# Prompt scores of a differential attention: one 128-row matmul against zero-padded queries, or two 64-row tiles of the array in turn

## What is computed

```python
scale = HEAD_DIM ** -0.5                          # HEAD_DIM = 64, N_SUB = 8, N_HEADS = 4
s = jnp.einsum('bqhd,bkhd->bhqk', q_blk, k, preferred_element_type=jnp.float32) * scale
s = jnp.where(k_pos[None, :] <= q_pos[:, None], s, -jnp.inf)
p = jax.nn.softmax(s, axis=-1)                    # per sub-head
a = p[:, :, 0] - lam * p[:, :, 1]                 # the two sub-heads of a head
out = jnp.einsum('bhqk,bkhe->bqhe', a, v)         # v: 4 heads of 128
```

## Time and profile before

| | |
|---|---|
| median of 3 runs | 1545.1 us (1535.18, 1545.1, 1546.49) |
| span of the profiled execution, first to last instruction | 1539.1 us |
| PE busy | 1306.9 us, 85% of the span |
| PE weight loads busy | 883.9 us, 57% |
| DVE busy | 744.7 us, 48% |
| ACT busy | 568.3 us, 37% |
| POOL busy | 283.7 us, 18% |
| mean granted TensorE clock | 0.937 of full speed |

### The profile page before, as it was taken

The page is one execution under the profiler, slowest core; times in us unless marked ns, Lnnn a source line. Parts: engine busy times, 40 slices in busy tenths (PEclk is TensorE's granted clock), DMA queues, the critical chain, the costliest instruction groups (busy, mean ns, idle before and its releaser), DMA issues.

```text
span 1539.1 us, 20098 instructions
## 1 busy us (share of the span) xinstructions
PE 1306.9 (85%) x5769; PEld 883.9 (57%) x5770; DVE 744.7 (48%) x1101; ACT 568.3 (37%) x786; POOL 283.7 (18%) x289
## 2 busy tenths in 40 slices
PE   4879999999997799789999899638989989899920
PEld 1334444366665466566565688426767777677720
DVE  4863232201113887511011454567865556888747
ACT  4530111000001556422232122206755546777633
POOL 0020000010000111000000011112554344554424
PEclk9989999999998999999999899758999999999965
DMA  8981200011100200077664311406875765888545
GB/s 288 367 318 32 82 28 26 16 46 42 41 0 0 84 1 1 1 233 237 193 173 126 127 41 42 183 16 247 303 269 200 272 251 218 313 303 324 216 157 184
DMA packets 84544, 230.86 MB, mean 150 GB/s; under 512 B 16101, under 2 KB 28517, under 8 KB 72165
## 3 DMA queue, kind: packets, MB, share of 16 engines
q1 hardware_dynamic: 70288, 203.80, 37.6%
q0 software_dynamic: 14192, 26.24, 4.8%
HBM read 220.42 MB, written 34.21 MB: 165 GB/s over the span
## 4 chain that ended last, share of the span: by engine, by line
PE 64%; DVE 10%; DMA 9%; issue 7%; ACT 5%; POOL 2%; DVEq 2%; ACTq 1%; SPq 1%; POOLq 0%
PE psum L530 19%; PE psum L583 12%; PE psum L611 11%; PE psum L690 4%; DMA xg<-h_scratch,gidx 4%; PE psum L517 4%; PE psum L705 2%; PE psum L629 2%; DMA wada<-in_w_ada_dram 2%; PE psum L638 2%; DVE xgL L1493 1%; ACT pexp L922 1%; DVEq L332 1%; PE psum L672 1%; DMA wgu<-in_w_up_dram 1%
## 5 line engine op out<-in xcount | busy, mean ns | idle before, releaser
L583 PE MATMUL psum<-wqkv,hT 128*128 128x512 f32 (+1 forms) x432 | 187.5, 594 | 0.0
L611 PE MATMUL psum<-hT,wcv 128*128 128x352 f32 x576 | 170.9, 459 | 0.0
L1485 DVE TENSOR_TENSOR wguL<-wgu,wguH 128x2048 fp32r<-128x2048 f32 x64 | 146.7, 2294 | 39.9 <-ACT wguH L1034 39.2
L530 PE MATMUL psum<-wguH,xgH 128*128 128x512 f32 x320 | 130.8, 409 | 33.0 <-DVE xgL L1493 33.0
L611 PEld LDWEIGHTS psum<-hT,wcv 128*128 128x128 f32 x576 | 109.3, 190 | 60.6
L583 PEld LDWEIGHTS psum<-wqkv,hT 128*128 128x128 f32 (+1 forms) x432 | 77.8, 182 | 103.2 <-issue 103.1
L1034 ACT CAST wguH<-wgu 128x2048 fp32r<-128x2048 f32 x64 | 120.3, 1912 | 23.5 <-issue 14.2
L530 PE MATMUL psum<-wguH,xgL 128*128 128x512 f32 x320 | 126.7, 396 | 0.0
L530 PE MATMUL psum<-wguL,xgH 128*128 128x512 f32 x320 | 126.4, 395 | 0.0
L1553 POOL TENSOR_SCALAR small<-small 128x1 f32<-128x1 f32 (+3 forms) x36 | 20.1, 559 | 508.4 <-ACT ajunk L1011 213.5
L629 PE MATMUL psum<-kT,qz 128*128 128x512 f32 (+3 forms) x192 | 77.7, 520 | 19.5 <-ACT pexp L922 18.2
(11 more groups left out here) (269 smaller groups left out, 2412.1 us busy)
## 6 DMA issues: line engine op xcount, KB each, us to landing
wgu<-in_w_gate_dram SPq DMA_DIRECT2D x32, 1024.0 KB, 4.9
wgu<-in_w_up_dram SPq DMA_DIRECT2D x32, 1024.0 KB, 7.5
wdn<-in_w_down_dram SPq DMA_DIRECT2D x32, 1024.0 KB, 7.4
wada<-in_w_ada_dram SPq DMA_DIRECT2D x24, 1024.0 KB, 8.2
kseq<-in_cache_k_dram SPq DMA_DIRECT2D x64, 256.0 KB, 3.0
vseq<-in_cache_v_dram SPq DMA_DIRECT2D x64, 256.0 KB
yg<-y_scratch SPq DMA_DIRECT2D x16, 512.0 KB, 4.9
wqkv<-in_w_in_dram SPq DMA_DIRECT2D x1, 6144.0 KB, 25.3
```

The costliest lines, as they stand in the source:

```text
L530: ins = mm(out, r32(x(c)), r32(w(c)), start=(begin and c == 0 and k == 0), stop=(end and c == chunks - 1 and k == 2))
L583: last = mm(psum[0:n, 2 + j, :], hT[:, c, P * t:P * t + n], wqkv[:, c, AW * j:AW * j + AW], start=(c == 0), stop=(c == DC - 1))
L611: last = mm(psum[:, 3 * (n % 2) + j, 0:TB], wcv[i % 2][:, c, j, :], hT[:, c, TB * tb:TB * tb + TB], start=(c == 0), stop=(c == DC - 1))
L1485: TT(r32(wguL[slot][:, g, :, :]), wgu[slot][:, g, :, :], wguH[slot][:, g, :, :], ALU.subtract).then_inc(S["wguL_done"], 1)
```

## The change

The queries are no longer padded: `qz` and the work on POOL that fills it are gone. A score matmul takes the 64 rows of its own sub-head from `qT` and `kT`, that is rows 0 to 63 of the array for u = 0 and rows 64 to 127 for u = 1. Both sub-heads now come from one call, `scores(w)`, key piece by key piece with the two sub-heads in turn, and the call waits once, for both exponentials of the step before, where the two calls waited for one each.

```diff
-        qz = [at(f"qz{i}", O_AB + 4 * K * i, [P, 2, HEADS, P]) for i in range(2)]
...
-            def scores(w, u):
+            def scores(w):
                 i, h = divmod(w, HEADS)
-                if w == 0 and u == 0:
-                    pe.wait_ge(W["qz_done"], 1)
-                elif h == 0 and u == 0:
-                    pe.wait_ge(W["qz_done"], i + 1)
                 if w >= 1:
-                    pe.wait_ge(W["exp_done"], 2 * w + u - 1)
+                    pe.wait_ge(W["exp_done"], 2 * w)
                 nk = P * (i + 1)
                 for a in range(0, nk, 512):
                     b = min(nk, a + 512)
-                    last = mm(psum[:, 2 * u + a // 512, 0:b - a], qz[i % 2][:, u, h, :], kT[:, h, a:b], start=True, stop=True)
-                last.then_inc(S["s_ps"], 1)
+                    for u in range(2):
+                        r = slice(64 * u, 64 * u + 64)
+                        last = mm(psum[:, 2 * u + a // 512, 0:b - a], qT[r, h, P * i:P * i + P], kT[r, h, a:b], start=True, stop=True)
+                        if b == nk:
+                            last.then_inc(S["s_ps"], 1)
...
-            scores(0, 0)
-            scores(0, 1)
+            pe.wait_ge(W["qT_sb"], NT)
+            scores(0)
             for w in range(8 * HEADS):
                 i, h = divmod(w, HEADS)
                 if w + 1 < 8 * HEADS:
-                    scores(w + 1, 0)
-                    scores(w + 1, 1)
+                    scores(w + 1)
...
-            def pad_queries(i):
-
-                if i >= 2:
-                    pool.wait_ge(W["s_ps"], 8 * (i - 1))
-                link(nc.gpsimd.tensor_copy(qz[i % 2][0:64, 0, :, :], qT[0:64, :, P * i:P * i + P]))
-                nc.gpsimd.tensor_copy(qz[i % 2][64:P, 1, :, :], qT[64:P, :, P * i:P * i + P]).then_inc(S["qz_done"], 1)
-                pool.wait_ge(W["qz_done"], i + 1)
...
             for i in range(8):
-                if i + 2 < 8:
-                    if i >= 1:
-                        pool.wait_ge(W["rstdh_done"], i)
-                    pad_queries(i + 2)
+                if i >= 1:
+                    pool.wait_ge(W["rstdh_done"], i)
                 pool.wait_ge(W["ssqh_done"], 4 * i + 4)
```

More of the change, by code:

```diff
@@ L286, in build @@
         cv_ps gates_sb cu_done conv_done nc_ps nc_sb nc_out ncT_done
-        qz_done s_ps mask_done nmax_done exp_done adiff_done adT_ps adT_sb o_ps ssqh_done rstdh_done att_done attT_ps attT_sb
+        s_ps mask_done nmax_done exp_done adiff_done adT_ps adT_sb o_ps ssqh_done rstdh_done att_done attT_ps attT_sb
         dscore_ps page_in kseq_in0 kseq_in1 kseq_in2 vseq_in0 vseq_in1 kp_ps kp_sb qbd_done ds_ps dnew_done dmax_done dexp_done pair_done
```

## The result

The changed kernel takes 1604.6 us (median of 4 runs, 1599.2 to 1607.4) against 1545.8 us for the kernel before (4 runs, 1535.2 to 1551.2): **slower by 3.8%**, ratio 1.038 with an interval of 1.033 to 1.044. The span of the profiled execution went from 1539.1 to 1597.4 us, +58.3. All of it but 1.5 us lies in one stretch, the one that the prediction summed: from the end of the second exponential of step 0 to that of step 31. It took 144.3 us and now takes 201.0. Its first part, "blocks 0 to 3", ends with the second exponential of step 16.

A forecast was written before the change was run, and what follows sets the result against it. No engine was full over the prompt attention stage; chains of waits set its steps. Joined chains +37.4, `qbd` fill +0.5 and clock +12 gave about +50 us, forecast 1595; own range 1583 to 1609, 8 in 10 range 1583 to 1620.

The forecast's parts named there:

- So the two chains are laid end to end: Prompt attention steps: the single wait joins both chains; a step grows from 6.85 to 8.59 us (block 7), 2.63 to 3.82 (block 1).
- the line: Step time by block in the prompt attention: 3.03 us for block 0 and 0.795 us more for each further block.
- The sum for the full clock: Second exponential of step 0 to that of step 31: 181.7 us after against 144.3 before, plus 0.5 for filling `qbd`.
- The rival on the other side: No loss worth the name: `adiff` doesn't wait for the next scores; +7 us, 1552, within 1% of before; chance 0.05.
- One sign that was named: In the prompt attention stage, ACT idle for transposes far more than the 39 us of before.
- the rival without overlap: Score matmuls of the two row tiles run one after the other; 13.6 us more from block 4 on, 1609; chance 0.33.
- The clock term: PE's clock rises later or falls in the new stage's pauses: 12 us taken, floor 0, 45 for all of blocks 1 to 7.
- +37.4 and +0.5: Prompt attention: +37.4 us from the joined chains between steps 0 and 31, +0.5 us from filling `qbd`.
- Overlap: Matmuls of the two row tiles run side by side, likelier case; otherwise 0.85 us a step in 16 steps, 13.6 us.
- Rows set no duration here.: Score matmuls on PE: time is paid by columns, 0.21 us for 128 keys and two instructions, so half the rows gain nothing.
- Changing the tile.: PE changes tiling mode twice a step, at most 0.13 us each; taken as 0, 8 us if on the path.
- POOL and the pieces once a block.: Dropping POOL's 16 copies and four clears: 0. Squares, inverse root and scaled rows hidden in DVE's wait: 0, otherwise +8 us.

The follow-up runs named there:

- the extra matmuls: The changed kernel plus full 128-row matmuls with overwritten results in TensorE's pauses, in 27 of 32 steps; ratio 1.033 to the kernel before, stretch 187.6 us.
- sub-head major version: The changed kernel with all score pieces of sub-head 0 ahead of those of sub-head 1; one run, 1606.5 us, stretch 202.7 us.
- version with `adiff` first: The changed kernel with VectorE's `adiff` of step w ahead of maxima(w+1, 0), single wait kept; ratio 1.005 to the kernel before, stretch 158.3 us.
- split version: 64-row tiles without padding, but the two calls and two waits of the kernel before; ratio 1.011 to that kernel, stretch 159.7 us.
- the pair with one bank: The kernel before (padded, two waits; stretch 144.3 us) and its variant with 64-row tiles and the same two waits (ratio 1.011, stretch 159.7 us).
- the pair with two: Kernel before with two score banks in turn in blocks 0 to 3 and scaled rows later: 64-row tiles there (ratio 1.003) against padded queries (0.991).
- kernel with padded scores in two banks: The kernel before with two score banks in turn in blocks 0 to 3 and scaled rows one step later, queries still padded; ratio 0.991, stretch 141.7 us.
- tiles version with later rows: The kernel before with 64-row tiles and two score banks in turn in blocks 0 to 3, scaled rows one step later; ratio 1.003, stretch 147.2 us.

## Why the prediction was right

**The mechanism and its size.** "So the two chains are laid end to end" holds link by link: the step in block 5 is 7.04 us against 7.0 by the line, and cutting the one link that the prediction named (`adiff` behind maxima(w+1, 0)) gives 43 us back. The sum for the full clock, 182.2 us, stands against 187.6 us in the version whose clock was held at 0.94 and 0.96, and 4.3 us of the difference are the three steps in which that clock fell. The rival on the other side, which needed this order to be misread, is excluded by the run that moves `adiff`. One sign that was named did not come: ACT was to wait for transposes far more than 39 us, and it waited 42.4. In the closed ring the transposes follow `adiff` as closely as before; what ACT waits for is the maximum of the next scores, 83.5 us.

**What the time alone doesn't tell.** 1604.6 us lies 9.6 us from the forecast of 1595 and only 4.4 from the 1609 of the rival without overlap. It is the trace that decides between them, by the 1.56 us of eight score instructions and the mask 1.59 us after the first of them (2.02 in block 7's one step with scores at the full clock, where "about 2.0" was named). The clock term was 7 us too small, and the number by itself would have spoken for the wrong rival.

**The clock, the term that was mis-sized.** I took 12 us and said it could be 0 to 45. With +37.4 and +0.5 as summed, the trace leaves 56.8 - 37.9 = 19 us for it, and the extra matmuls gave 13.4 of them back. The seven us between are most of what the forecast of 1595 lacks to 1604.6; the rest is the other stages (+1.5) and the spread of the median. The step of the argument that was thin: I read from 510 to 515 that the clock holds with TensorE busy for 3.0 of 5 us, and took the new ring to be like that. In the kernel after the clock stayed at half until 540, 39 us longer than before. Two things go with that, and the runs don't weigh them: the pauses of the ring (padded scores with one wait had the clock up at 522, 28 us after step 0) and the 64-row scores (with two waits, up at 541). Chance has a part too: the sub-head major version, with the same ring, had it up 32 us after step 0, where the kernel after took 48.

**Overlap.** Taken as the likelier case, and right: no block pays the 0.85 us of the serial case. My picture of it was too small, though: in the rival on the other side I gave the two halves 5 slots of 0.43 us, and they take 4 (1.99 us for eight in block 7 of the version with `adiff` first). The page TensorE: Matmul & The Clock Gate of the Trainium skill, Part 3, which reports row tiles running together, agrees with this trace: 1.56 us for eight instructions. The strict order of starts that the prediction cites from it is not what the sub-head major version shows, where the tiles start in pairs against the program order.

**"Rows set no duration here."** True for the instruction, not for the kernel. With two waits and tiles, blocks 0 to 3 took 70.7 us instead of 58.2, with the clock at half for 55 us of them instead of 10, and that alone is 12.5 us. The prediction had no term for it; that its clock term covered part of it was luck, since this cause wasn't in it.

**Changing the tile.** Taken as 0, bounded by 8 us. The split version pays 89.0 instead of 86.1 us in blocks 4 to 7 at the full clock, 0.19 us a step; the first weighted values start 1.91 us after the second half of the scores, 1.83 before. It isn't parted from other effects. In the kernel after the change ahead of the weighted values is hidden, as said: TensorE stands idle for 1.51 us behind them in the step of block 5.

**POOL and the pieces once a block.** POOL waited 190.9 us for the same row as before (184.5), so nothing was gained there, as said. That the squares and scaled rows are hidden in the new ring was argued only; no run takes them out of it.

## What to carry to other kernels

A wait that is merged with another one, or a loop that is turned so that two halves go together, has to be followed round the ring of engines: list what each engine has in its program between the late arrival and the next item that others need. Here up to 2 us less of TensorE work a step was paid with 1.2 to 1.7 us more for everybody by the sum, and the place of `adiff` on VectorE decided most of it. And when TensorE's load is cut in a stage that isn't bound by it, look at the granted clock in the rows before and after: the time saved can be given back by everything else that TensorE runs there.

## What the runs showed of the hardware

- Two float32 matmuls on row tiles 0 to 63 and 64 to 127 start 6 to 13 ns apart and run together at full rate; eight took 1.56 us where eight serial ones of the same size took 2.85, and it made no difference whether they alternate in the program or stand one sub-head after the other.
- At the start of the stage the clock came up later with scores of 64 rows than with zero-padded scores of 128 rows in the same order, with the same waits and as many score instructions: 48 against 10 us after the end of step 0 in the pair with one bank (541 and 501), 24 against 8 in the pair with two (517 and 505). In the first pair's tiles version it was at 0.50 from 495 to 540 with TensorE busy for 44.75 of 45 us. Half of the padded operand is zeros, so zeros did not keep the clock down.
- That is shown for the start of this stage by two pairs of traces, not more, and it is no rule: in blocks 4 to 7 scores of 64 rows ran at 1.00 for 89 us (TensorE busy for 84.57), and padded scores of 128 rows in the ring with one wait stayed at 0.50 for 28 us (busy for 19.94).
- What stays open: the kernel with padded scores in two banks is 13 us faster by its ratio, of which its stretch explains 2.6. In its trace 891.5 us follow the stretch, against 903.4 in the trace of before; there the clock fell once between 676 and 976 us; in the trace of before it fell nine times between 676 and 877. The trace of the tiles version with later rows looks the same (889.3 us), but it is of an execution of 1532 us, its fastest, where the median of that version is 1549. So such a quiet late part is not the new order's own. Five of the ten executions of the padded version were under 1534 us, one of twelve of that tiles version, none of fifteen of before beside them and three of twenty-nine in an earlier set. Whether the new order brings it more often, these runs don't tell.
